# Adding the old value to the inverse on VectorE instead of in its PSUM bank

## The reference, cut to what matters

```python
def step(S, inp):
    r_t, w_t, k_t, v_t, kk_t, a_t = inp
    sa = -jnp.einsum('dbhvk,dbhk->dbhv', S, kk_t)
    S = (S * w_t[..., None, :] + sa[..., :, None] * (kk_t * a_t)[..., None, :]
         + v_t[..., :, None] * k_t[..., None, :])
    return S, jnp.einsum('dbhvk,dbhk->dbhv', S, r_t)
```

## Time and profile before

| | us |
|---|---|
| median of 3 runs | 2977.77 (2973.8, 2977.77, 2983.11) |
| profiled execution, its own time | 2975.01 |
| span of the profiled execution | 2973.2 |
| RWKV levels, first to last start of a level product | 455.5 to 708.3 |

### The profile page before, as it was taken

The page is one execution under the profiler, slowest core; times in us unless marked ns, Lnnn a source line. Parts: engine busy times, 40 slices in busy tenths (PEclk is TensorE's granted clock), DMA queues, the critical chain, the costliest instruction groups (busy, mean ns, idle before and its releaser), DMA issues. The chain is left out here.

```text
span 2973.2 us, 43857 instructions
## 1 busy us (share of the span) xinstructions
PE 2692.7 (91%) x18304; PEld 2243.0 (75%) x18304; DVE 1947.8 (66%) x1851; ACT 1148.7 (39%) x1313; POOL 259.1 (9%) x175
## 2 busy tenths in 40 slices
PE   1599979998698999999999779996889999999997
PEld 1488868997487888888888667885768888888885
DVE  7786636775656777787877768437467845555557
ACT  0343335553444333333333333338443333333332
POOL 0000000000004000000000047412013000000000
PEclk9999989998899999999999899999999999999998
DMA  9798821210264887888888358550448855555552
GB/s 353 290 364 303 314 90 55 84 64 32 105 220 159 310 310 295 304 319 296 319 304 319 110 218 312 182 183 1 171 150 328 299 170 194 186 187 194 185 196 85
DMA packets 256964, 636.33 MB, mean 214 GB/s; under 512 B 10222, under 2 KB 17060, under 8 KB 234692
## 3 DMA queue, kind: packets, MB, share of 16 engines
q1 hardware_dynamic: 250674, 621.77, 58.6%
q10 hardware_dynamic: 6162, 12.72, 1.1%
HBM read 632.35 MB, written 2.10 MB: 213 GB/s over the span
## 5 line engine op out<-in xcount | busy, mean ns | idle before, releaser
L448 DVE TENSOR_TENSOR s_wl<-s_raw,s_wh 128x2048 fp32r<-128x2048 f32 (+1 forms) x396 | 929.3, 2347 | 667.2 <-ACT s_wh L443 665.4
L443 ACT ACTIVATE s_wh<-s_raw 128x2048 fp32r<-128x2048 f32 (+1 forms) x396 | 758.3, 1915 | 1271.1 <-PE pa L543 614.2
L541 PE MATMUL pa<-s_wh,s_hth 128*128 128x512 f32 (+1 forms) x1760 | 704.7, 400 | 39.0 <-DVE s_wl L448 16.4
L542 PE MATMUL pa<-s_wl,s_hth 128*128 128x512 f32 (+1 forms) x1760 | 695.0, 395 | 0.0
L543 PE MATMUL pa<-s_wh,s_htl 128*128 128x512 f32 (+1 forms) x1760 | 694.1, 394 | 0.0
L541 PEld LDWEIGHTS pa<-s_wh,s_hth 128*128 128x128 f32 x1760 | 337.6, 192 | 123.3 <-DVE s_wl L448 20.7
L543 PEld LDWEIGHTS pa<-s_wh,s_htl 128*128 128x128 f32 x1760 | 336.5, 191 | 71.8
L542 PEld LDWEIGHTS pa<-s_wl,s_hth 128*128 128x128 f32 x1760 | 337.5, 192 | 67.3
L487 DVE SCALAR_TENSOR_TENSOR s_wide<-s_adaw,s_silu_c,s_wide 128x2048 f32<-128x2048 f32 x150 | 360.1, 2401 | 0.0
L541 PE MATMUL py<-s_wh,s_guh 128*128 128x512 f32 x704 | 276.9, 393 | 11.7 <-DVE s_ysum L936 11.7
L543 PE MATMUL py<-s_wh,s_gul 128*128 128x512 f32 x704 | 275.5, 391 | 0.0
(11 more groups left out here) (329 smaller groups left out, 2405.3 us busy)
## 6 DMA issues: line engine op xcount, KB each, us to landing
s_raw<-in_ffn_w_in SPq DMA_DIRECT2D x176, 1024.0 KB, 5.3
s_adaw<-in_ada_w SPq DMA_DIRECT2D x160, 1024.0 KB, 5.6
s_raw<-in_ffn_w_out SPq DMA_DIRECT2D x88, 1024.0 KB, 7.5
s_raw<-in_ab_w_in SPq DMA_DIRECT2D x48, 1024.0 KB, 7.6
s_raw<-in_diff_w_in SPq DMA_DIRECT2D x48, 1024.0 KB, 5.3
s_raw<-in_ada_w SPq DMA_DIRECT2D x32, 1024.0 KB, 7.6
s_raw<-in_ab_w_out SPq DMA_DIRECT2D x16, 1024.0 KB, 5.2
s_raw<-in_diff_w_out SPq DMA_DIRECT2D x16, 1024.0 KB, 5.1
```

The costliest lines, as they stand in the source:

```text
L443: act.activation(wh[:, s % 2, :, 0:width], raw[:, s, :, 0:width], ACT.Copy).then_inc(hi_done, 1)
L448: dve.tensor_tensor(wl[:, s % 2, :, 0:width], raw[:, s, :, 0:width], wh[:, s % 2, :, 0:width].bitcast(F32), ALU.subtract).then_inc(lo_done, 1)
L541: pe.matmul(o, a_hi, w_hi, start=start and k == 0, stop=False)
L542: pe.matmul(o, a_hi, w_lo, start=False, stop=False)
```

## The change

The inverse no longer adds up in L3. PE's `first` does not write L3, PE's `level_w` writes its product alone (`start=(u == 0)`), and VectorE reads the bank and adds the old `R_W` on the way to `R_W` or `R_WF`. ScalarE's copy is gone. L2 still adds up as before. On VectorE `level_w(t, 1)` to `(t, 4)` stand ahead of `level_q(t, 2)` to `(t, 5)`, and `level_w(t, 5)` stands between the two `masked` and `first`.

```diff
-            def level_w(t, lv):                       # ScalarE
-                act.wait_ge(w_done, 5 * t + lv)
-                act.activation(flat(R_WF if lv == LEVELS - 1 else R_W), L3, ACT.Copy).then_inc(wc_ready, 1)
...
+            def level_w(t, lv):                       # VectorE
+                dve.wait_ge(w_done, 5 * t + lv)
+                dve.tensor_tensor(flat(R_WF if lv == LEVELS - 1 else R_W), flat(R_W), L3, ALU.add).then_inc(wc_ready, 1)
...
                 if lev:
+                    level_w(t, 1)
                     level_q(t, 2)
...
                 if lev:
+                    level_w(t, 2)
                     level_q(t, 3)
                     masked(t, 3)
...
                 if lev:
+                    level_w(t, 3)
                     level_q(t, 4)
                 if front:
                     unit_keys(n)
                     factors(n)
                 if lev:
+                    level_w(t, 4)
                     level_q(t, 5)
                 if front:
                     masked(n, 0)
                     masked(n, 1)
+                if lev:
+                    level_w(t, 5)
+                if front:
                     first(n)
...
                 mm.then_inc(v_done, 1)                # PE, first(n)
-                if n:
-                    pe.wait_ge(wc_ready, 5 * n)
-                for u in range(NU):
-                    two(unit(L3, u), eye2, R_W[:, u], start=(u == 0))
...
                 pe.wait_ge(qc_ready, 5 * t + lv)      # PE, level_w(t, lv)
-                if lv > 1:
+                if 5 * t + lv > 1:
                     pe.wait_ge(wc_ready, 5 * t + lv - 1)
                 for u in range(NU):
-                    mm = two(unit(L3, u), R_Q[:, u], R_W[:, u])
+                    mm = two(unit(L3, u), R_Q[:, u], R_W[:, u], start=(u == 0))
                 mm.then_inc(w_done, 1)
```

More of the change, by code:

```diff
@@ L1399, in _ @@
                         load_up(m)
-                if lev:
-                    level_w(t, 1)
                 if front:
@@ L1409, in _ @@
                     chain_u(c, 1)
-                if lev:
-                    level_w(t, 2)
                 if front:
@@ L1423, in _ @@
                     norm_exp(n)
-                if lev:
-                    level_w(t, 3)
                 if front:
@@ L1438, in _ @@
                     turned_ab(t, 1)
-                    level_w(t, 4)
                     turned_v(t)
-                    level_w(t, 5)
                 if t == PAIRS:
```

## The result

The changed kernel takes 2984.1 us (median of 20 runs, 2976.45 to 2989.91), the kernel before 2977.93 in as many runs beside it. The ratio is 1.0020, with a 95% interval of 1.0012 to 1.0028: 6 us slower, where 1.1 was forecast. The time lies in the range, and the difference is under the 0.3% that the prediction took for the smallest that can be told; the interval says that it is a small loss all the same. The profiled execution has a span of 2984.7 us (before: 2973.2), 11.5 us more. 7.07 of them have come by the end of the RWKV stage and are followed up here; the other 4.4 lie behind it.

What follows compares the result with a forecast made beforehand. PE's order was taken as the bound. Terms of 0 for PE's group, 0 for ScalarE and 0.24 + 0.90 for VectorE gave +1.1 us on the median 2977.77, so 2978.9 us; range 2971 to 2986.

Steps and rivals of the forecast that it cites:

- PE's group is worth nothing: Removing `first`'s L3 writing, 0.93 us at 8 pairs, saves 0, because PE then idles waiting for ScalarE's copy of `R_V`.
- ScalarE's copies are worth nothing: Dropping ScalarE's 40 copies to `R_W` and `R_WF` saves 0, since PE waits for none of its results there.
- An addition takes 0.69 us: Each of VectorE's 40 new additions of bank and SBUF tile takes 0.69 us, between 0.60 and 1.38.
- Levels 1 to 4 covered: VectorE's additions at levels 1 to 4 fit into idle time or behind PE's own work; cost 0.
- Level 5 makes VectorE 0.90 us late, with 0.2 us of cover in iterations 2 to 6: The addition delays `first` by 0.90 us; the next level 1 mask is 0.65 us late, still covered; cost 0.
- 0.24 us in iteration 1's `first`, 0.90 in iteration 7: `R_W` ready late for PE's `first` costs 0.24 us; iteration 7's wait for the level 1 mask grows 0.90 us.
- Rival C, the clock: Iteration 7's longer PE wait halves the clock, costing 2 to 4 us more, 2981 to 2983 us; chance 0.20.
- throw of the dice: By the skill's free-running clock gate, whether the clock falls in iteration 7 is chance in each run.
- the comparison with the earlier trace: Iteration 7's wait of 2.64 us lies nearly at a 3.4 us stretch followed by half clock; 1.7 us left it full.

Runs made afterwards that it cites:

- E1: The changed kernel with PE's `first` writing `R_W` into bank L3 again, products that nothing reads; 2985.67 us in a single execution.
- E9: The changed kernel with one more VectorE pass of 128x512, its result unread, behind `level_w(t, 5)`; 2989.42 us in a single execution.
- E2: The changed kernel with 14 of the stage's 16 conditioning loads left out, passes computing on old data; 2982.37 us in a single execution.
- E6: The changed kernel with each burst's second conditioning load held until VectorE's mask of level 2 is done; 2988.92 us in a single execution.
- E3: The kernel before with 14 of the stage's 16 conditioning loads left out; 2975.01 us in a single execution.
- E8: The changed kernel with `cond_step` moved behind iteration 7's mask, loads apart, PE's `first` earlier, `level_w(t, 5)` inside VectorE's `first`, `square` before `load_up`; 2971.69 us, 0.9985.
- E10: The kernel before with iteration 6's second `cond_step` behind iteration 7's level 1 mask, and each burst's second load delayed; 2980.33 us, 1.0010.

## Why the prediction was right, and what it missed

- *PE's group is worth nothing*: right for its time. Idle of 0.70 us (0.93 had been said) takes its place, and 0.08 us a pair at most is gained (E1).
- *ScalarE's copies are worth nothing*: right; no wait of PE went with them.
- *An addition takes 0.69 us*: 0.68 to 0.69. The Trainium skill's rule (VectorE: DVE Perf Modes, The TRN2 errata) of 62 cycles more for a PSUM source does not show: 681 ns with a bank as one source, 692 without.
- *Levels 1 to 4 covered*: right, idle left 0.00, 0.55 and 0.61 us.
- *Level 5 makes VectorE 0.90 us late, with 0.2 us of cover in iterations 2 to 6*: right, no wait there; E9 measures 0.28 for the cover.
- *0.24 us in iteration 1's `first`, 0.90 in iteration 7*: right, 0.27 and 0.92.
- *Rival C, the clock*: it happened. I gave it 0.20 with 2 to 4 us, and it cost 2.7. Windows around the wait in the changed kernel, columns as in the earlier trace rows, with the clock third from the end:

```profile
687.80:691.00 3.20, 0.61 (x22) 0.47 (x17) 3.12 (x5) 0.28 (x1) 2.77 (x1) 0.87 0.73 297
691.10:694.50 3.40, 3.40 (x64) 3.40 (x66) 0.00 (x0) 0.77 (x2) 0.20 (x1) 0.50 0.87 294
694.50:697.00 2.50, 2.50 (x42) 2.50 (x40) 0.90 (x5) 0.00 (x0) 0.00 (x0) 0.50 0.14 52
...
691.09 1.97 PE L2048 MATMUL pt<-s_R_Q,s_R_W 64*64 64x64 f32 x32 [2.69 <-DVE s_R_Q L1677]
```

The product of 1.15 us took 1.97, at 1.2 GHz. In the traces with a wait of 2.66 us or more (after, E1, E2, E6, E9) the clock fell each time; with 1.74 (before, E3) or 0.56 us (the other six) it fell in none. So whether it falls was no throw of the dice, and the chance should have gone by the comparison with the earlier trace rows that stood in the prediction. How long it stays low did vary: from the product behind the wait to the level 5 product 2.7 us are lost in the changed kernel and 2.3 in E9, but 1.5 to 1.6 in E1, E2 and E6, where it was low for about half as long. The Trainium skill (TensorE: Matmul & The Clock Gate, What's actually happening) has the gate look in free-running stretches; that much agrees, since the product right behind the wait already took 1.97 us in three of the five and still 1.15 in E2 and E6.

- *What failed*: the sum had a step for each engine and none for what stands between them. "PE's group: 0" was right for its time, but with the group 0.25 blocks of code an iteration went too, and 2.5 us of gaps in iterations 1 to 5 came with it, which the term had at nothing. The trace of before held the hint, an iteration of 33.87 us with an unexplained "issue" of PE in it, and I read it as no part of the change. Another 0.25 us is ScalarE's load issue in iteration 0.

The terms 0.27 + 0.92 + 2.7 + 2.5 + 0.25 + 0.44 make the 7.07 us of the stage in the profiled execution, to 0.01; the medians differ by 6.2. With the forecast's own terms at 1.2 us, the mechanism priced in the sum was right and two others were the larger part. That 2984.1 us lies in the range is owed to its upper end, which was rival C and half the spread of the runs, and in part to luck: the gaps were in no rival. That the gaps need the burst is shown (E2, E3, E6). That they come from code fetched behind it fits the starts of the q8 blocks, with and without loads, and the counts of 28 and 29, but nothing moved the blocks alone, and it stays argued. The 0.44 us ahead of the stage, the 4.4 behind it and E6's excess stay open.

## What to carry to other kernels

An operation that fills a wait is worth nothing until the wait's other end moves: here removing it paid only with E8's moves, about 0.55 us a pair. Look at the longest existing wait on TensorE first: 0.9 us added to one that stood at 1.74 cost 1.5 to 2.7 us more by the clock, and one moved pass took it back. And after any change of the instruction count, look for "issue" gaps that come once an iteration: here they needed the large loads, and both a change of the count (E1) and a move of the loads (E6, E10) shifted them.

## What the runs showed of the hardware

- TensorE stood for 0.15 to 1.39 us with nothing to wait for, shortly behind a burst of two 1 MB loads at whose end a code block started; in the changed kernel it did not with one load at a time or none (E2, E6). With one load at a time it still did in E10, for up to 0.83 us, and once in E8, for 0.29. The Trainium skill (Runtime: NRT & Kernel Launch, Instruction fetch mechanics) says that each engine refills its code in 16 KiB blocks by a DMA queue of its own, and that crossing a block is mostly hidden. The rows of q8 agree on the size (28 blocks, 0.46 MB); that it is hidden holds here without the loads (E2, E3), and not always beside them.
- A DMA issue on ScalarE took 0.47 us in one kernel and 1.43 in the other at the same place (line 1223 in iteration 0), and held an activation behind it. It is no property of the change: in iterations 1 to 5 the same line took 0.88 to 1.68 us in the kernel before and 0.47 to 0.48 in the changed one. The changed kernel's rows:

```profile
462.09 1.43 ACTq L1223 DMA_DIRECT2D s_raw<-in_rwkv_a_up  x1
...
464.11 0.51 ACT L1266 ACTIVATE s_R_sq<-s_R_rk,s_neg 128x256 f32<-128x256 f32 x1 [1.26 <-issue]
```
